# The order of the steps of attention: one turning of probabilities behind each bank of scores, third and fourth exponentials apart

## The chip, the core and the metric

One core of a Trainium2 chip. The metric is the time of one execution on the device in microseconds, median of several runs: 1551.44 us (1549.46 to 1552.54 in 3 runs). The granted TensorE clock over the span was 0.988 of full speed.

## What is computed

One inference step of a hybrid layer over 2048 prompt positions (and 128 sample positions): RMSNorm, one wide input projection, three mixers side by side (forgetting attention of 8 heads x 64, an S5 state space, memory attention of 4 heads x 64 into 256 tokens), each gated, and an output projection with a residual. The change touches only the attention of the prompt:

```
def fox_block(q, k, v, cq, ck, q_pos, k_pos):
    s = einsum('bqhd,bkhd->bhqk', q, k) * HEAD_DIM ** -0.5
    s = s + cq[..., :, None] - ck[..., None, :]          # decay of the forget gates
    p = softmax(where(k_pos[None, :] <= q_pos[:, None], s, -inf))
    return einsum('bhqk,bkhd->bqhd', p, v)
```

and the memory attention, which is the same without decay and mask. All of it is in float32 or in pairs of rounded float32 parts.

## The kernel before

`before_attention` (projections, S5, the sample positions) takes the span up to about 819 us. `attention_and_output` then runs attention to about 1348 us and the output projection to the end.

**Rounds.** A head's 16 query tiles of 128 rows are cut into 11 *rounds* (`attention_rounds`, L1859); 8 heads make 88, numbered through. In heads 0 to 6 the rounds have, in this order, query tile 12; 13; 14; 15; 8 with memory tiles 0 and 1; 9 with 2 and 3; 10 with 4 and 5; 11 with 6 and 7; 0 to 3; 4 and 5; 6 and 7. The last head (`LAST_GROUPS`) begins with the small tiles. So rounds 11 to 14 are tiles 12 to 15 of the second head, 15 to 18 its tiles 8 to 11, 19 to 21 the small ones, and 22 begins the third head. Tile t has t+1 key blocks of 128 (the mask leaves out the rest). Every round has 4 *banks* of scores, a bank being up to 4 key blocks (128x512); the blocks are then turned (transposed) in 3 or 4 *turnings* of up to 4 blocks. Rounds are paired into groups (the small ones are three), 5 per head and 40 in all, and each group's products with the values are made at once.

**Steps.** I write S(n,i) for the scores of bank i of round n, E(n,i) for its exponentials, T(n,i) for a turning, V for a group's products with the values, B for the turning back of a group's output.

- S(n,i), TensorE: L2202 and L2205, for the diagonal block L2204; for memory L2208 and L2209. It writes one of 5 banks of PSUM (`RING`), so it waits for E of five banks before: S(n,1) waits for E(n-1,0), S(n,2) for E(n-1,1), S(n,3) for E(n-1,2), S(n+1,0) for E(n-1,3). VectorE reduces each bank to its maximum (L2367) and, when a tile's banks are through, makes the negated maximum (L2371; L2360 and L2363 where one bank is all). So where a tile fills all four banks (rounds 11 to 14, and 22 on), E(n,0) cannot begin before the maximum of S(n,3); in rounds 15 to 18 it follows the third bank.
- E(n,i), ScalarE: L2291, with a row sum that is read out by a second instruction.
- T(n,i), TensorE: L2219, four transposes into one of 2 banks (`TURNS`), so it waits until the turning two before it is copied out. The copies alternate through the whole stage: even ones on ScalarE (L2301), odd ones on VectorE (L2380); rounds 19 and 20 have 3 turnings, so in round 20 the two engines change parts. So T(n-1,0) waits for ScalarE's copy of T(n-2,2), T(n-2,3) for VectorE's of T(n-2,1).
- V (L2235) on TensorE, its copy (L2307) on ScalarE, B (L2242) on TensorE, the division by the sums (L2390, L2393, L2402) on VectorE.

**The order.** `attention_order` (L1875) writes one list of steps. Each engine walks that list and takes its own part of each step, in order, with semaphore waits in front: an instruction that waits holds everything behind it on its engine. A step of scores is TensorE's matmuls and VectorE's maximum; a turning is TensorE's transposes and the copy on ScalarE or VectorE. Per iteration n the list before is

```
S(n,0) E(n-1,2) E(n-1,3) T(n-2,2) T(n-2,3) [B] [V] S(n,1) S(n,2) T(n-1,0) S(n,3) T(n-1,1) E(n,0) E(n,1)
```

V comes in the iteration three after its group's last round, B in the one after that. In the last head ScalarE also rounds the output weights, one piece ahead of T(n-1,0) and one behind E(n,1). Behind attention come the output projection's steps (`mix`, `mixed`, `product`, `y`), which the change does not touch. DMAs are issued by SyncE alone, and none is in this list; they wait for semaphores of attention's progress.

Of the kernel before, what the change touches and what calls it, by code (L numbers as in the profile page):

```python
# [1874 lines left out]
def attention_order(rounds):  # L1875


    last = {n: r.group for n, r in enumerate(rounds) if n + 1 == len(rounds) or rounds[n + 1].group != r.group}
    order = []

    def some(what, n, at):
        if 0 <= n < len(rounds):
            have = len(rounds[n].turns if what == "turn" else rounds[n].banks)
            order.extend((what, n, i) for i in at if i < have)

    first = next(n for n, r in enumerate(rounds) if r.head == FOX_HEADS - 1)
    for n in range(len(rounds) + 4):
        some("scores", n, (0,))
        some("exp", n - 1, (2, 3))
        some("turn", n - 2, (2, 3))  # L1890
        if n - 4 in last:
            order.append(("back", last[n - 4]))
        if n - 3 in last:
            order.append(("values", last[n - 3]))
        if first < n <= first + KC:
            order.append(("w_split", n - first - 1, 0))
        some("scores", n, (1, 2))
        some("turn", n - 1, (0,))
        some("scores", n, (3,))
        some("turn", n - 1, (1,))  # L1900
        some("exp", n, (0, 1))
        if first < n <= first + KC:
            order.append(("w_split", n - first - 1, 1))


        if n == len(rounds) + 1:
            order.append(("mix", 0))
            order.append(("mixed", 0))
        if n == len(rounds) + 2:
            order.append(("product", 0, 0))  # L1910
            order.append(("mix", 1))
    order += [("mixed", 1), ("product", 0, 1), ("y", 0, 0), ("y", 0, 1)]
    for o in range(1, TILES):
        order.append(("product", o, 0))
        if o + 1 < TILES:
            order += [("mix", o + 1), ("mixed", o + 1)]
        order += [("product", o, 1), ("y", o, 0), ("y", o, 1)]
    return order


def attention_and_output(nc, K, D, w_out):
# [9 lines left out]
    LANE = HD + 2  # L1931
    rounds, groups = attention_rounds()
    order = attention_order(rounds)
    SLOTS = max(sum(len(r.blocks) for r in g) for g in groups)
    bank0, turn0 = ([sum(len(x(r)) for r in rounds[:n]) for n in range(len(rounds) + 1)]
# [586 lines left out]
```

## Time and profile before

| | |
|---|---|
| median of 3 runs | 1551.44 us |
| profiled execution | 1551.53 us, of it span 1549.8 us |
| TensorE busy in the span | 1453.9 us, 94% |
| VectorE busy | 863.9 us, 56% |
| ScalarE busy | 712.5 us, 46% |

Times in rows are microseconds from the start of the span. A row of the timeline is a run of like instructions on one engine: start, time until the last one ends, engine, line, operation, the tiles written and read, shape, count, and in brackets how long the engine stood idle before it and whose result ended the idle time. A matmul's end is modelled, and matmuls overlap: four transposes take 0.60 us from the first start to the last end, but the next matmul starts 0.35 us after the first. So waits between TensorE's steps are best read from start to start.

### The profile page before, as it was taken

Reading aid. Unit: us, or ns where it says so; the run is one execution under the profiler, and the core shown is the slowest. Engines: PE = TensorE matmul, PEld = TensorE weight load, DVE = VectorE, ACT = ScalarE, POOL = GpSimd, SP = SyncE. Lnnn points to the kernel's source line nnn. Section 1 sums busy time; section 2 is a strip of 40 time slices with the busy share of each in tenths; the row PEclk is TensorE's granted clock in tenths of the full one; section 3 lists DMA queues with packets and bytes.
Section 4 is the critical chain, followed back from the end, with each engine's and each line's share of the span. In section 5 each row is a group of like instructions: output and inputs, shape, how many; then the busy total and the mean of one; then the engine's idle time right before and its main releaser. Section 6 shows DMA issues by size and latency. Waiting matters only on the chain. (4 is left out here: it accounts for less than half of the span.)

```text
span 1549.8 us, 28675 instructions
## 1 busy us (share of the span) xinstructions
PE 1453.9 (94%) x10318; PEld 1196.5 (77%) x10318; DVE 863.9 (56%) x1873; ACT 712.5 (46%) x1726; POOL 215.4 (14%) x294
## 2 busy tenths in 40 slices
PE   7999997999989989999997999999999999899998
PEld 7998766778767767777776777877778787788887
DVE  3689754772557776663325666666666665422221
ACT  5666422432524543453325665666666667500100
POOL 1110442100133332220001000000000003221110
PEclk9999998999999999999998999999999999999999
DMA  7785799695398596779868545062451602155543
GB/s 223 237 268 202 253 251 238 204 310 171 96 251 270 184 264 218 258 247 329 271 202 190 158 87 124 22 144 53 92 117 29 144 2 63 56 177 174 183 153 105
DMA packets 207676, 271.86 MB, mean 175 GB/s; under 512 B 73456, under 2 KB 147600, under 8 KB 203920
## 3 DMA queue, kind: packets, MB, share of 16 engines
q1 hardware_dynamic: 206496, 270.02, 59.7%
q8 instruction: 84, 1.38, 0.4%
q14 instruction: 56, 0.46, 0.1%
q10 hardware_dynamic: 1040, 0.00, 0.0%
HBM read 184.83 MB, written 83.90 MB: 173 GB/s over the span
## 5 line engine op out<-in xcount | busy, mean ns | idle before, releaser
L910 PE MATMUL in_g<-in_wh,in_xh 128*128 128x512 f32 (+2 forms) x904 | 333.8, 382 | 16.3 <-DVE in_wl L1478 5.8
L910 PE MATMUL in_g<-in_wl,in_xh 128*128 128x512 f32 (+2 forms) x904 | 323.3, 371 | 0.0
L2367 DVE TENSOR_REDUCE attn_tops<-attn_s 128x1 f32<-128x512 f32 (+3 forms) x288 | 171.5, 618 | 142.5 <-PE attn_s L2205 141.4
L2291 ACT ACTIVATE attn_probs<-attn_s,attn_negmax 128x512 f32<-128x512 f32 (+3 forms) x384 | 224.3, 601 | 30.9 <-DVE attn_negmax L2371 30.9
L910 PE MATMUL in_g<-in_wh,in_xl 128*128 128x512 f32 (+2 forms) x904 | 236.3, 380 | 1.4 <-DVE in_xl L1502 1.3
L2219 PE MATMUL attn_t<-all_ident,attn_probs 128*128 128x128 f32 x1216 | 192.9, 278 | 36.0 <-ACT attn_probs_turned L2301 21.9
L910 PEld LDWEIGHTS in_g<-in_wh,in_xh 128*128 128x128 f32 x904 | 166.5, 190 | 53.9 <-issue 21.1
L2219 PEld LDWEIGHTS attn_t<-all_ident,attn_probs 128*128 128x128 f32 x1216 | 144.5, 142 | 79.3 <-issue 31.2
L910 PEld LDWEIGHTS in_g<-in_wl,in_xh 128*128 128x128 f32 x904 | 166.7, 190 | 28.3
L910 PEld LDWEIGHTS in_g<-in_wh,in_xl 128*128 128x128 f32 x904 | 159.1, 190 | 34.9 <-issue 5.2
L2301 ACT ACTIVATE attn_probs_turned<-attn_t 128x512 f32<-128x512 f32 x168 | 99.9, 594 | 83.4 <-PE attn_t L2219 83.4
L2235 PE MATMUL attn_pv<-attn_probs_turned,attn_v 128*64 128x128 f32 x2176 | 134.6, 275 | 0.9 <-DVE attn_out L2402 0.7
L2235 PEld LDWEIGHTS attn_pv<-attn_probs_turned,attn_v 128*64 128x64 f32 x2176 | 125.1, 137 | 7.1 <-issue 5.6
L1196 ACT ACTIVATE in_xh<-in_xu 128x512 fp32r<-128x512 f32 x174 | 99.6, 622 | 43.3 <-DMA in_xu<-scratch_xt 38.0
L2380 DVE COPY attn_probs_turned<-attn_t 128x512 f32<-128x512 f32 (+3 forms) x168 | 100.5, 598 | 14.4 <-PE attn_t L2219 12.7
L2268 PE MATMUL attn_s<-wout_lo,attn_qa 128*128 128x512 f32 x272 | 106.0, 390 | 0.0
L2327 ACT ACTIVATE attn_qa<-attn_s 128x512 fp32r<-128x512 f32 (+1 forms) x34 | 14.8, 488 | 162.3 <-PE attn_s L2254 162.3
L1780 POOL TENSOR_TENSOR in_hv<-in_hs,all_neghalf 128x8 f32<-128x8 f32 (+1 forms) x53 | 85.9, 1620 | 4.4
L1502 DVE TENSOR_TENSOR in_xl<-in_xu,in_xh 128x512 fp32r<-128x512 f32 x106 | 68.6, 688 | 25.7 <-ACT in_xh L1196 25.5
L2291 ACT ACTIVATION_READ_ACCUMULATOR attn_probs<-attn_s,attn_negmax 128x1 f32 x384 | 80.1, 209 | 0.0
L1778 POOL TENSOR_SCALAR in_hs<-in_hs 128x8 f32<-128x8 f32 (+1 forms) x53 | 22.2, 419 | 407.7 <-DVE in_hs L1529 407.7
L2202 PE MATMUL attn_s<-all_ka,all_qa 128*128 128x512 f32 (+3 forms) x160 | 70.9, 443 | 7.6 <-PEq L72 6.4
(288 smaller groups left out, 2337.7 us busy)
## 6 DMA issues: line engine op xcount, KB each, us to landing
in_xu<-scratch_xt SPq DMA_DIRECT2D x87, 512.0 KB, 4.8
in_xl<-scratch_xt SPq DMA_DIRECT2D x34, 512.0 KB, 4.6
in_raw<-in_w_in SPq DMA_DIRECT2D x40, 256.0 KB, 5.5
scratch_xt<-in_xu SPq DMA_DIRECT2D x19, 512.0 KB, 5.3
scratch_xt<-in_xl SPq DMA_DIRECT2D x17, 512.0 KB, 6.2
scratch_k<-in_x_turned SPq DMA_DIRECT2D x17, 512.0 KB, 6.0
scratch_q<-in_x_turned SPq DMA_DIRECT2D x17, 512.0 KB, 5.3
in_x_turned<-in_x_prompt SPq DMA_DIRECT2D x16, 512.0 KB, 4.9
```

Of the source, the lines that this page charges most:

```text
L910: last = X.matmul(g_ps[b][:, 0:m], x, ws[:, c, w0:w0 + m], start=(c == 0 and h == 0 and ws is wh), stop=(c == KC - 1 and h == 1))
L1196: F(xh[:, item_visit[j] % 2, 4 * h:4 * h + 4, :], xu[:, j % 2, 4 * h:4 * h + 4, :], ACT.Copy)\
L1502: V.tensor_tensor(xl[:, v % 3, 4 * h:4 * h + 4, :], xu[:, j % 2, 4 * h:4 * h + 4, :], fl(xh[:, v % 2, 4 * h:4 * h + 4, :]), ALU.subtract). ...
L1780: G.tensor_tensor(hv[:, 0:m], hs[:, 0:m], K.neghalf[:, 0:m], ALU.pow).then_inc(s_hchain, 1)
L2202: X.matmul(bank[:, at:at + n, :], qa[h][:, q], ka[h][:, keys], start=True, stop=False)
L2219: last = X.transpose(t_ps[q % TURNS][:, j, :], probs[:, s % 2, i, at, :], K.ident[:, :])
L2235: last = X.matmul(v_ps[lane * HD:(lane + 1) * HD, j, :], vals[:, k, :], pt[:, s % 2, slots[lane, k], :], start=k == 0, stop=(lane, k + 1) ...
L2268: last = X.matmul(y_ps[h], ms[:, o % 2, c, :], ws, start=(c == 0 and k == 0), stop=(c == KC - 1 and k == 2))
L2291: last = F(probs[:, s % 2, i, at:at + n, :], s_ps[g % RING][:, at:at + n, :], ACT.Exp, bias=negmax[:, s % 2, top:top + 1], accum_out=total)
L2301: F(pt[:, r.group % 2, at:at + n, :], t_ps[q % TURNS][:, 0:n, :], ACT.Copy).then_inc(s_read_a, 1)
L2367: V.tensor_reduce(tops[:, s % 2, i:i + 1], bank[:, 0:n, :].rearrange("p n k -> p (n k)"), AX.X, ALU.max).then_inc(s_top, 1)
L2380: V.tensor_copy(pt[:, r.group % 2, at:at + n, :], t_ps[q % TURNS][:, 0:n, :]).then_inc(s_read_v, 1)
```

## The change

```diff
@@ def attention_order(rounds):
     for n in range(len(rounds) + 4):
         some("scores", n, (0,))
-        some("exp", n - 1, (2, 3))
-        some("turn", n - 2, (2, 3))
+        some("exp", n - 1, (2,))
+        some("turn", n - 2, (2,))
+        some("scores", n, (1,))
+        some("exp", n - 1, (3,))
+        some("turn", n - 2, (3,))
         if n - 4 in last:
             order.append(("back", last[n - 4]))
         if n - 3 in last:
             order.append(("values", last[n - 3]))
         if first < n <= first + KC:
             order.append(("w_split", n - first - 1, 0))
-        some("scores", n, (1, 2))
+        some("scores", n, (2,))
         some("turn", n - 1, (0,))
         some("scores", n, (3,))
         some("turn", n - 1, (1,))
```

The list of an iteration becomes

```
S(n,0) E(n-1,2) T(n-2,2) S(n,1) E(n-1,3) T(n-2,3) [B] [V] S(n,2) T(n-1,0) S(n,3) T(n-1,1) E(n,0) E(n,1)
```

On TensorE S(n,1) moves ahead of T(n-2,3), B and V. On ScalarE the copy of T(n-2,2) moves ahead of E(n-1,3). On VectorE the maximum of S(n,1) moves ahead of the copy of T(n-2,3) and of B's division. No instruction is added or taken away, and no wait's condition changes.

## Rows read from the trace of the kernel before

**Rows 1.** The page: busy time by engine; TensorE in 40 slices; its group of turnings

```profile
PE 1453.9 (94%) x10318; PEld 1196.5 (77%) x10318; DVE 863.9 (56%) x1873; ACT 712.5 (46%) x1726; POOL 215.4 (14%) x294
...
PE   7999997999989989999997999999999999899998
...
L2219 PE MATMUL attn_t<-all_ident,attn_probs 128*128 128x128 f32 x1216 | 192.9, 278 | 36.0 <-ACT attn_probs_turned L2301 21.9
```

**Rows 2.** Stretches: length; busy (count) of PE, PEld, DVE, ACT, POOL; clock; DMA

```profile
840.00:1340.00 500.00, 463.78 (x4479) 390.08 (x4476) 316.97 (x718) 328.49 (x956) 20.84 (x10) 1.00 0.39 88
905.00:970.00 65.00, 60.34 (x583) 50.68 (x584) 41.54 (x95) 41.87 (x124) 0.00 (x0) 1.00 0.41 88
```

**Rows 3.** TensorE's waits, 840 to 1340 us: us in total, times, longest

```profile
PE attn_t L2219 <- ACT attn_probs_turned L2301: 20.3, 30, 1.7
PE attn_t L2219 <- DVE attn_probs_turned L2380: 9.4, 27, 0.8
PE attn_s L2202 <- ACT attn_probs L2291: 1.7, 7, 0.3
```

**Rows 4.** Timeline, end of iteration 14 and iteration 15, up to V

```profile
902.03 0.47 PE L2202 MATMUL attn_s<-attn_ka,attn_qa 128*128 128x512 f32 x1
...
902.71 0.60 PE L2219 MATMUL attn_t<-all_ident,attn_probs 128*128 128x128 f32 x4
...
902.90 0.69 DVE L2367 TENSOR_REDUCE attn_tops<-attn_s 128x1 f32<-128x512 f32 x1 [0.75 <-PE attn_s L2205]
...
903.06 0.48 PE L2202 MATMUL attn_s<-attn_ka,attn_qa 128*128 128x512 f32 x1
...
903.61 0.60 PE L2219 MATMUL attn_t<-all_ident,attn_probs 128*128 128x128 f32 x4
...
903.82 0.69 ACT L2291 ACTIVATE attn_probs<-attn_s,attn_negmax 128x512 f32<-128x512 f32 x1 [0.92 <-DVE attn_negmax L2371]
...
904.41 0.19 ACT L2291 ACTIVATION_READ_ACCUMULATOR attn_probs<-attn_s,attn_negmax 128x1 f32 x1
...
904.55 0.52 PE L2219 MATMUL attn_t<-all_ident,attn_probs 128*128 128x128 f32 x3 [0.33 <-DVE attn_probs_turned L2380]
...
905.00 3.28 PE L2235 MATMUL attn_pv<-attn_probs_turned,attn_v 128*64 128x128 f32 x54
```

**Rows 5.** Timeline, iterations 16 and 17, up to V

```profile
910.18 0.68 ACT L2291 ACTIVATE attn_probs<-attn_s,attn_negmax 128x512 f32<-128x512 f32 x1
...
910.88 1.36 PE L2219 MATMUL attn_t<-all_ident,attn_probs 128*128 128x128 f32 x8
...
911.85 0.49 ACT L2291 ACTIVATE attn_probs<-attn_s,attn_negmax 128x256 f32<-128x256 f32 x1
...
912.28 0.69 DVE L2380 COPY attn_probs_turned<-attn_t 128x512 f32<-128x512 f32 x1 [0.21 <-PE attn_t L2219]
...
912.66 0.28 PE L2202 MATMUL attn_s<-attn_ka,attn_qa 128*128 128x256 f32 x1
...
912.75 0.62 ACT L2301 ACTIVATE attn_probs_turned<-attn_t 128x512 f32<-128x512 f32 x1
...
913.52 0.63 PE L2219 MATMUL attn_t<-all_ident,attn_probs 128*128 128x128 f32 x4 [0.34 <-ACT attn_probs_turned L2301]
...
914.72 0.69 ACT L2291 ACTIVATE attn_probs<-attn_s,attn_negmax 128x512 f32<-128x512 f32 x1
...
916.34 3.71 PE L2235 MATMUL attn_pv<-attn_probs_turned,attn_v 128*64 128x128 f32 x62
```

**Rows 6.** Timeline of TensorE, two further waits of this head

```profile
925.70 0.63 PE L2219 MATMUL attn_t<-all_ident,attn_probs 128*128 128x128 f32 x4 [0.53 <-ACT attn_probs_turned L2301]
...
946.88 0.51 PE L2202 MATMUL attn_s<-all_ka,all_qa 128*128 128x512 f32 x1 [0.23 <-ACT attn_probs L2291]
```

**Rows 7.** TensorE's longest wait of the stage, on the timeline

```profile
1294.02 0.98 PE L2219 MATMUL attn_t<-all_ident,attn_probs 128*128 128x128 f32 x4 [1.73 <-ACT attn_probs_turned L2301]
```

**Rows 8.** The stretch behind that wait, columns as in rows 2

```profile
1294.00:1297.40 3.40, 3.38 (x15) 3.10 (x16) 1.34 (x2) 2.76 (x8) 0.56 (x1) 0.52 0.20 80
```

## The prediction

> **What bounds the kernel now.** The page comes first: TensorE is busy 94% of the span, VectorE 56%, ScalarE 46% [rows 1]. Attention's steady part, 840 to 1340 us, is 463.8 of 500 us busy on TensorE at full clock, against 317 and 328 us on the other two [rows 2]. So TensorE is the bound, and what an order of steps can win is the time in which it stands. The table of waits says what it stands for: 20.3 us in 30 waits of a turning for ScalarE's copy, 9.4 us in 27 for VectorE's copy, and only 1.7 us of scores waiting for exponentials [rows 3]. A matmul's modelled end hides part of every wait: the turning of 913.52 is listed with 0.34 us idle, yet the scores before it begin at 912.66 and fill 0.28 us, so it is 0.58 us late [rows 5]. Four turnings take 0.60 us [rows 4] and one lasts 0.28 [rows 1], so they follow each other at (0.60 - 0.28) / 3 = 0.11 us; the eight at 910.88 should take 7 x 0.11 + 0.28 = 1.05 us and take 1.36, so a wait of 0.3 us hides there with no bracket at all [rows 5]. One head period, 905 to 970, holds by such starts about 7.5 us of standing, though its busy sum leaves only 4.7 us [rows 2]. That 7.5 us is an estimate from reading every step's start once round the head.
>
> The Trainium skill, Perfetto Trace Analysis, section Identifying the Most-Contended Engine, warns that matmul occupancy is no good measure of what TensorE has left. The trace agrees: 7.5 against 4.7 us in this head. By the busy sum alone all eight heads would have 37 us to give, by the starts 60 us; neither is my sum, which comes from the walk below.
>
> **The change part by part.** Every instruction stays; three moves are made, and none is a DMA's. SyncE's queue and POOL's are not in the list and are not passed; their waits fall earlier with attention's progress.
>
> *Move 1, ScalarE's copy of T(n-2,2) ahead of E(n-1,3).* In iteration 16, E(15,3) starts at 911.85 (two exponentials of 256) and the copy of T(14,2) only at 912.75; it ends at 913.37 and T(15,0) starts 0.15 us later [rows 5]. Moved, the copy starts at 911.87 and ends at 912.48, so T(15,0) may start at 912.63, 0.9 us earlier. With one bank of 512 in E(n-1,3), the move is worth one exponential, 0.69 us [rows 4]. E(15,3) ends where the copy ended before; its takers, S(17,0) and T(15,3), come three steps later on TensorE, so nothing waits. ScalarE is now held by the copy if the turning is late, but T(14,2) is done about 0.4 us before the copy is due, and in none of the walks below is it late.
>
> *Move 2, S(n,1) ahead of T(n-2,3).* This gives VectorE time to copy T(n-2,1), which is the 0.3 us in the row of eight and the 0.33 us of 904.55 [rows 4, 5]. But S(n,1) needs the bank that E(n-1,0) reads. Before, T(n-2,3), B and V stood between, and V alone is 3.2 us (54 products, 3.28 us to the last one's end [rows 4]). Now only S(n,0) and T(n-2,2) do. Where a tile fills four banks the chain is: S(14,3) at 902.03, its maximum from 902.90, E(14,0) 903.82 to 904.60 [rows 4]. TensorE would be ready for S(15,1) at 903.61 + 0.38 = 903.99 and gets its bank at 904.65: a new wait of 0.66 us, in place of the old one, which ended at 904.55.
>
> *Move 3, on VectorE,* the maximum of S(n,1) goes ahead of the copy of T(n-2,3) and the division behind B. The work is the same, begun earlier; S(n,2)'s maximum now follows the division, which I put at 1.1 us for a group of eight tiles (an estimate: one pass over 128x512, 0.69 us as the maximum of 902.90 [rows 4], and two short ones ahead), and E(n,0) follows that.
>
> *The walk, V to V.* V is long enough for ScalarE and VectorE to empty their queues, so each stretch between two V can be walked alone, and the results added. I take the rows' times, put the steps in the new order, and let each start at the latest of: the step before it on its engine (a bank of 512 scores 0.55 us, from 903.06 to 903.61; four turnings 0.35, from 902.71 to 903.06, to 0.38 before scores, 4 x 0.11 before turnings [rows 4]), the copy's end + 0.15 [rows 5], the exponential's end + 0.05 (my estimate for a wait that the rows barely show).
>
> Stretch of iterations 16 and 17 [rows 5]. T(14,2) at 910.88. S(16,1) could start at 911.26; E(15,0), from 910.18, ends with its read-out 0.78 us later (as 903.82 to 904.60 [rows 4]), at 910.96, so it does. T(14,3) 911.81, B, S(16,2) 912.30, T(15,0) 912.63 rather than 913.52. VectorE: the maximum of S(16,1) begins 0.77 us after its start (0.87 from 902.03 to 902.90 less the 0.10 of the diagonal block [rows 4]), at 912.03, then copy, division and maximum of S(16,2) follow without a gap, the same work that before began at 912.28; so E(16,0) starts at 914.5 rather than 914.72 and ends at 915.28. TensorE: S(16,3) 913.0, T(15,1) 913.57, S(17,0) 913.93, T(15,2) 914.48; ready at 914.86, S(17,1) waits until 915.33. T(15,3) 915.88, V 916.12 rather than 916.34. S(17,1) is already done, which took 0.57 us behind V before. Gain 0.22 + 0.57 = 0.8 us. So 0.9 us are freed at T(15,0) and 0.3 at T(14,3), and 0.47 us are lost again at S(17,1).
>
> Stretch of iterations 14 and 15. S(14,3), at 902.03 in rows 4, comes 0.55 us earlier, but VectorE, with a division of 1.1 us between, makes E(14,0) only 0.3 us earlier, 903.5 to 904.3. S(15,1) 904.33, T(13,3) 904.88, V 905.33, its successor S(15,2) at 905.33 + 3.2 = 908.53, where before it stood at 905.00 + 3.2 + 0.57 = 908.77: gain 0.25 us. Each head has one such stretch.
>
> The other three, walked alike: iterations 18 and 19, where T(17,0) waits for ScalarE at 925.70 [rows 6], gain 1.1; 20 and 21, 0.45; 22 to 24, about -0.1. In the last, B and V stood before S(22,1), which still started only when E(21,0) was done (946.88 [rows 6]); now B's 0.33 us comes behind that wait instead of within it, and the later waits win 0.27 us back.
>
> Sum per head 0.8 + 0.25 + 1.1 + 0.45 - 0.1 = 2.5 us. Of the 7.5 us of standing, 5 stay, 4.3 of it in front of S(·,1). Eight heads: 20 us; I take 2.45, the unrounded sum, so 19.6 us. The last head has other neighbours but the same round shapes. Behind attention TensorE is busy 8 to 9 tenths of every slice with the output projection [rows 1], and its loads wait for attention's own semaphores, so the gain passes through.
>
> Against the profiled execution, 1551.5 us (0.1 above the median of 1551.44), this is 1531.9. I forecast **1532 us**.
>
> Bounds. Above: if all listed waits went, 31.4 us [rows 3], and the half clock of 1294 to 1297.4 too. There TensorE stood 1.73 us for ScalarE's copy behind two exponentials of 256 and ran 3.4 us at 0.52 of its clock [rows 7, 8]; the copy now comes 0.9 us earlier. That is worth at most half of 3.4, 1.7 us. I do not count it, and do not expect the whole of the waits; low end 1524. Below: the rivals.
>
> **Rivals.**
>
> *A, the forecast:* 1532 us, chance 0.60.
>
> *B, the wait only changes its place.* The bank of E(n-1,0) sets the pace everywhere as it does in iteration 15, and the earlier copy merely lets TensorE reach S(n,1) sooner. For it: E(14,0) already waits 0.92 us on its maximum [rows 4]. Against: in iterations 16 to 21 E(n,0) hangs on the third bank and on ScalarE's queue, which move 1 shortens. Then each V stretch wins what 14 and 15 win or less, 0.15: 40 stretches, 6 us: 1545.5. Chance 0.22.
>
> *C, slower: S(n,1) in front of V starves TensorE.* V used to cover the chain S(n-1,3), maximum, E(n-1,0). Now five times per head TensorE must sit it out before V may begin, and VectorE's division makes the chain longer in the iterations with B. My walk has 4.3 us of such waits per head, 0.39 per iteration. From 6.75 us per head, 0.61 per iteration, the change loses. The 0.66 us of iteration 15 lies on that side, and so does any VectorE that comes 0.3 us later than walked. At 0.67 us per iteration in all 88: 88 x 0.06 = 5 us slower, 1556.5. Chance 0.10.
>
> *D, the clock.* A long stand cost half clock once, at 1294 [rows 7, 8]; the other 29 of that kind, 0.64 us each in the mean, did not: (20.3 - 1.7) / 29 [rows 3]. If the new waits before S(n,1), up to 1 us in iteration 26, set it off, each costs up to 1.7 us. The Trainium skill, TensorE: Matmul & The Clock Gate, section A second HAM failure mode, describes just this, short idle gaps between groups that cycle PSUM banks; here the clock held at 1.00 through 500 us with 57 listed waits on turnings [rows 2, 3]. Six such falls: 10 us given back, 1542; twelve would eat the gain. Chance 0.08.
>
> That the change does not do what it says (the copy held by a late T(n-2,2)) would be B's time.
>
> **How the numbers follow.** About 0.2%, 3.1 us, is what a measurement of this kernel can tell from no change. Faster by more: all of A, most of B (0.19 of 0.22), most of D (0.06): 0.85. The same: 0.05. Slower: 0.10, C. The range runs from 1524 to 1547: it takes in B and most of D, and leaves out C and a gain of over 27 us.
>
> **What would show it.** T waiting for ScalarE's copy falls from 20.3 us to under 6; T waiting for VectorE's from 9.4 to under 3; S waiting for exponentials rises from 1.7 to 15 to 30 us. Attention, 529 us before (819 to 1348), would take about 509, and no other stretch changes its length. The prediction is wrong in its step if S's waits exceed 40 us, or if the clock falls below 1.00 in new places.

## The result and the profile after

The changed kernel takes 1533.69 us (median; 1531.68 to 1535.54, 4 runs) against 1551.45 for the kernel before (4 runs): ratio 0.9884, 95% interval 0.9864 to 0.9904, 17.8 us faster. On another chip, in a later comparison, it was 1531.18 against 1548.48: 0.9887 (0.987 to 0.9903). The forecast was 1532 us, with a range of 1524 to 1547.

The page of the changed kernel first: busy time by engine, TensorE in 40 slices, and the group of turnings, which answer to rows 1.

```profile
PE 1452.1 (95%) x10318; PEld 1199.1 (78%) x10318; DVE 860.7 (56%) x1873; ACT 714.0 (47%) x1726; POOL 216.8 (14%) x294
...
PE   7999997999998989999997999999999999999998
...
L2223 PE MATMUL attn_t<-all_ident,attn_probs 128*128 128x128 f32 x1216 | 190.7, 275 | 5.8 <-ACT attn_probs_turned L2305 4.3
```

No engine has fewer instructions; the turnings' listed idle time fell from 36.0 us [rows 1] to 5.8. (The lines of `kernel.py` stand 4 lower after the change: L2206 and L2209 are scores, L2223 turnings, L2239 V.) TensorE's waits in 840 to 1340 us, as in rows 3:

```profile
PE attn_s L2206 <- ACT attn_probs L2295: 17.0, 39, 0.8
PE attn_t L2223 <- ACT attn_probs_turned L2305: 3.8, 9, 0.7
PE attn_t L2223 <- DVE attn_probs_turned L2384: 0.9, 1, 0.9
```

Both waits on copies are nearly gone, 29.7 us to 4.7, and 17.0 us of scores waiting for exponentials stand in their place, in 39 waits where there were 7 [rows 3]. The granted clock was 1.00 throughout, with 475.7 of 500 us busy on TensorE where there were 463.8 [rows 2]:

```profile
840.00:1340.00 500.00, 475.67 (x4608) 403.92 (x4608) 320.14 (x734) 334.95 (x969) 22.83 (x12) 1.00 0.40 91
```

The timeline of the changed kernel shows where the new waits stand, here in iterations 14 and 15, which answer to rows 4:

```profile
900.33 0.15 DVE L2394 TENSOR_REDUCE attn_den<-attn_dens 128x4 f32<-128x8 f32 x1
...
900.75 0.69 DVE L2406 TENSOR_TENSOR attn_out<-attn_pv,attn_rden 128x512 f32<-128x512 f32 x1
...
900.92 0.47 PE L2206 MATMUL attn_s<-attn_ka,attn_qa 128*128 128x512 f32 x1
...
901.36 1.28 DVE L2371 TENSOR_REDUCE attn_tops<-attn_s 128x1 f32<-128x512 f32 x2
...
902.67 0.16 DVE L2375 TENSOR_REDUCE attn_negmax<-attn_tops 128x1 f32<-128x4 f32 x1
...
902.87 0.69 ACT L2295 ACTIVATE attn_probs<-attn_s,attn_negmax 128x512 f32<-128x512 f32 x1 [1.06 <-DVE attn_negmax L2375]
...
903.70 0.50 PE L2206 MATMUL attn_s<-attn_ka,attn_qa 128*128 128x512 f32 x1 [0.60 <-ACT attn_probs L2295]
...
904.69 0.55 PE L2239 MATMUL attn_pv<-attn_probs_turned,attn_v 128*64 128x128 f32 x6
```

S(14,3) starts at 900.92 and its maximum could be taken 0.87 us later, at 901.79, as before [rows 4]. VectorE, held by the division (900.33 to 901.44) and then by the maximum of S(14,2), comes to it at about 901.96. E(14,0) follows at 902.87, and S(15,1) at 903.70, after 0.60 us of listed idle time, before V may begin. This profile's attention began 1.8 us later (S(0,0) at 820.65 us instead of 818.85), in work that the change does not touch. One stretch of that work, 3.4 us from 224.66, ran at half clock (0.50), which it did not in the profile before; why is open.

### The profile page after: what moved, and what is told of

It is laid out like the page before. It is cut to its first block and busy times, and to the rows that moved or that the text cites. A ratio compares the mean times of both kernels' runs of the same rounds, so it can differ in the third digit from the quotient of the medians.

```text
span 1533.7 us, 28675 instructions
## 1 busy us (share of the span) xinstructions
PE 1452.1 (95%) x10318; PEld 1199.1 (78%) x10318; DVE 860.7 (56%) x1873; ACT 714.0 (47%) x1726; POOL 216.8 (14%) x294
## 5 line engine op out<-in xcount | busy, mean ns | idle before, releaser
L2295 ACT ACTIVATE attn_probs<-attn_s,attn_negmax 128x512 f32<-128x512 f32 (+3 forms) x384 | 227.7, 605 | 38.5 <-DVE attn_negmax L2375 38.3
L2223 PE MATMUL attn_t<-all_ident,attn_probs 128*128 128x128 f32 x1216 | 190.7, 275 | 5.8 <-ACT attn_probs_turned L2305 4.3
L2223 PEld LDWEIGHTS attn_t<-all_ident,attn_probs 128*128 128x128 f32 x1216 | 147.3, 141 | 40.2 <-issue 9.2
L2239 PE MATMUL attn_pv<-attn_probs_turned,attn_v 128*64 128x128 f32 x2176 | 134.6, 275 | 0.8 <-DVE attn_out L2406 0.7
L2239 PEld LDWEIGHTS attn_pv<-attn_probs_turned,attn_v 128*64 128x64 f32 x2176 | 125.0, 137 | 8.7 <-issue 8.7
L2206 PE MATMUL attn_s<-all_ka,all_qa 128*128 128x512 f32 (+3 forms) x160 | 74.3, 464 | 16.0 <-ACT attn_probs L2295 9.2
L2206 PE MATMUL attn_s<-attn_ka,attn_qa 128*128 128x512 f32 (+3 forms) x160 | 72.6, 454 | 9.5 <-ACT attn_probs L2295 8.7
```

The lines of the kernel that those rows point to most:

```text
L2206: X.matmul(bank[:, at:at + n, :], qa[h][:, q], ka[h][:, keys], start=True, stop=False)
L2223: last = X.transpose(t_ps[q % TURNS][:, j, :], probs[:, s % 2, i, at, :], K.ident[:, :])
L2239: last = X.matmul(v_ps[lane * HD:(lane + 1) * HD, j, :], vals[:, k, :], pt[:, s % 2, slots[lane, k], :], start=k == 0, stop=(lane, k + 1) ...
L2295: last = F(probs[:, s % 2, i, at:at + n, :], s_ps[g % RING][:, at:at + n, :], ACT.Exp, bias=negmax[:, s % 2, top:top + 1], accum_out=total)
```

## The experiments

TensorE's own stretches tell more than the totals. The table gives, for each kernel, the distance in us from the start of S(n,2) of an iteration with a V to that of the next one, in the second to the sixth head, where it repeats to about 0.1 us (but for one stretch of d and one of f in the fifth head, which are left out here and told at the end); "one head" is their sum, the median and the ratio are of all comparable runs. The experiments ran on three chips, where the kernel before took 1550.07 (a to d), 1551.56 (e, f, g) and 1548.48 us (h, i), so the ratios, each to the kernel before on the same chip, compare better than the medians. Stretches are named by their iterations in the second head. For instance in the changed kernel S(15,2) and S(17,2) start at

```profile
907.89 0.33 PE L2206 MATMUL attn_s<-attn_ka,attn_qa 128*128 128x128 f32 x1
...
918.90 0.45 PE L2206 MATMUL attn_s<-attn_ka,attn_qa 128*128 128x384 f32 x1
```

and 918.90 - 907.89 = 11.01.

| kernel | 14-15 | 16-17 | 18-19 | 20-21 | 22-24 | one head | median | ratio to before (95%) |
|---|---|---|---|---|---|---|---|---|
| before | 12.81 | 11.77 | 11.86 | 11.00 | 17.42 | 64.86 | 1551.45 | 1 |
| the change | 12.59 | 11.01 | 10.96 | 10.81 | 17.55 | 62.92 | 1533.69 | 0.9884 (0.9864 to 0.9904) |
| a, copy only | 12.25 | 11.72 | 11.38 | 11.00 | 17.1 | 63.45 | 1540.24 | 0.9926 (0.991 to 0.9942) |
| b, scores only | 13.00 | 11.46 | 11.50 | 10.83 | 17.9 | 64.7 | 1545.78 | 0.9979 (0.9969 to 0.9989) |
| c, change, B late | 12.44 | 10.75 | 10.74 | 11.18 | 16.67 | 61.78 | 1525.25 | 0.9846 (0.9833 to 0.9859) |
| d, scores behind V | 12.42 | 11.42 | 11.31 | 10.70 | 17.38 | 63.23 | 1537.22 | 0.9917 (0.9906 to 0.9929) |
| e, before, B late | 13.40 | 12.13 | 12.01 | 11.98 | 16.85 | 66.37 | 1561.72 | 1.0075 (1.0063 to 1.0088) |
| f, mix | 12.83 | 10.64 | 10.73 | 10.80 | 16.55 | 61.55 | 1526.61 | 0.985 (0.9836 to 0.9864) |
| h, mix again | 12.41 | 10.64 | 10.74 | 10.78 | 16.55 | 61.1 | 1521.69 | 0.9826 (0.9811 to 0.9841) |

**a: ScalarE's copy alone.** Against the changed kernel:

```diff
         some("turn", n - 2, (2,))
-        some("scores", n, (1,))
         some("exp", n - 1, (3,))
...
-        some("scores", n, (2,))
+        some("scores", n, (1, 2))
```

> The changed kernel with S(n,1) back behind V: only ScalarE's copy of T(n-2,2) stays ahead of E(n-1,3). My theory (the waits are chained through VectorE, so the copy pays only where VectorE itself stood): walked alone per head, stretch 14-15 gains 0.7 us, 16-17 nothing (VectorE works without a gap from 912.28 to 915.96 in the kernel before, so T(15,3) and V stay where they were), 18-19 0.4, 20-21 nothing, 22-24 0.5; 1.6 us per head, about 13 us in all, 1538.5 us. T's waits for ScalarE's copy under 5 us, T's waits for VectorE's copy still about 9 us. Rival 'the copy is the whole change': as fast as the changed kernel, 1533 to 1534. Rival 'each move is worth its listed wait': 20 us, 1531.

1540.24 us, 9.8 below before on that chip (1550.07). The rival that the copy is the whole change (1533 to 1534) is out. The head gains 1.4 us where 1.6 was expected: 0.56, 0.05, 0.48, 0 and 0.3. T's waits went over to VectorE's copy; the third row is T(15,3):

```profile
PE attn_t L2222 <- DVE attn_probs_turned L2383: 15.9, 36, 0.8
PE attn_t L2222 <- ACT attn_probs_turned L2304: 7.0, 17, 0.8
...
919.00 0.30 PE L2222 MATMUL attn_t<-all_ident,attn_probs 128*128 128x128 f32 x1 [0.57 <-DVE attn_probs_turned L2383]
```

In 16-17 the copy of T(14,2) starts 0.9 us earlier behind S(15,2) than before. T(15,0) comes only 0.5 us earlier (4.25 us behind S(15,2), before 4.74), because it then waits for nothing but its place behind S(16,2). Nearly all of that is spent again at T(15,3). The wait on ScalarE came out a little above the 5 us expected, the one on VectorE well above 9, which is the chain through VectorE shown more plainly than I had asked.

**b: the scores alone.** Against the changed kernel:

```diff
-        some("exp", n - 1, (2,))
+        some("exp", n - 1, (2, 3))
         some("turn", n - 2, (2,))
         some("scores", n, (1,))
-        some("exp", n - 1, (3,))
         some("turn", n - 2, (3,))
```

> The changed kernel with E(n-1,2) and E(n-1,3) together again ahead of T(n-2,2): only S(n,1) ahead of T(n-2,3), B and V stays. My theory: T's wait for ScalarE's copy stays at about 20 us, the wait for VectorE's copy goes, S(n,1) waits for E(n-1,0). Walked per head: 14-15 loses 0.1, 16-17 gains 0.4, 18-19 0.6, 20-21 0.2, 22-24 loses 0.4: 0.7 us per head, 5 to 6 us in all, 1546. Rival C of the prediction (S(n,1) in front of V starves TensorE and only the copy pays): slower than before, 1552 to 1557. Rival 'each move is worth its listed wait': 9 us, 1542.

1545.78 us, 4.3 below before: close to the walk, and neither rival. By head it is only 0.2 us instead of 0.7, with the signs as walked (-0.2, 0.3, 0.4, 0.2, -0.5). The attention stage of its trace is 2.1 us shorter than before, so half of the 4.3 us was not found in the trace.

Alone the two moves give 1.4 and 0.2 us per head, together 1.94. The difference comes from 16-17, where they give 0.05 and 0.31 alone and 0.76 together; in 14-15 they give 0.15 less together than alone. The traces show why in 16-17: kernel a still waits at T(15,3) for VectorE's copy (0.57 us, above), kernel b at T(15,0) for ScalarE's,

```profile
912.28 0.63 PE L2222 MATMUL attn_t<-all_ident,attn_probs 128*128 128x128 f32 x4 [0.65 <-ACT attn_probs_turned L2304]
```

and the changed kernel has neither wait there.

**d: S(n,1) behind V.** Against the changed kernel, in iterations with a V only:

```diff
-        some("scores", n, (1,))
+        if n - 3 not in last:
+            some("scores", n, (1,))
...
             order.append(("values", last[n - 3]))
+        if n - 3 in last:
+            some("scores", n, (1,))
```

> The changed kernel, but in the iterations that have a V, S(n,1) goes behind V again (as in the kernel before); in the others it stays ahead of T(n-2,3). Tells whether the wait of S(n,1) in front of V costs or only stands in another's place. My theory: per head iteration 15 gains 0.1, 17 loses 0.25, 19 loses 0.45, 21 nothing, 24 gains 0.1; 0.5 us per head, 4 us slower than the changed kernel, about 1538. Rival C (V is needed as a cover for the chain to E(n-1,0)): faster than the changed kernel by 5 us or more.

1537.22 us, 3.5 slower than the change by the medians, 5 by the ratios to the kernel before (0.9917 against 0.9884 and 0.9887). Rival C is out: over a head, the wait of S(n,1) in front of V costs less than what stood there. Where the round before V is a large or a small one (14-15, 20-21, 22-24) S(n,1) is 0.1 to 0.2 us better behind V; where that round has memory tiles, 0.4 worse. The signs are as walked (20-21 was walked as nothing), the sum is 0.3 us per head instead of 0.5.

**c: B late.** Against the changed kernel:

```diff
-        if n - 4 in last:
-            order.append(("back", last[n - 4]))
...
         some("turn", n - 1, (1,))
+        if n - 4 in last:
+            order.append(("back", last[n - 4]))
         some("exp", n, (0, 1))
```

> The changed kernel with B (turning back of the output, and VectorE's division behind it) moved from ahead of V to behind T(n-1,1), so the division no longer stands between the maxima of S(n,1) and S(n,2). My theory says that in the changed kernel E(n,0) hangs on VectorE in the iterations with B, and S(n+1,1) on E(n,0). Walked: stretch 14-15 gains 0.3 us, 16-17 0.4, 18-19 0.4, 20-21 0.1, 22-24 0.5, so at most 1.7 us per head; since V may then wait for the division I expect two thirds of it, 9 us below the changed kernel, about 1525. S waiting for exponentials falls well under 17 us. Rival 'ScalarE's queue, not VectorE, sets E(n,0)': within 2 us of the changed kernel. Rival 'V waits for the division instead': slower than the changed kernel, V's waits for attn_out over 5 us.

1525.25 us. Taken by the ratios, 0.9846 against 0.9884 and 0.9887, that is 6 us below the change, not 9; the heads gain 1.14 us each, as two thirds of 1.7, but the last one loses 0.6. The waits of scores for exponentials fall to 7.1:

```profile
PE attn_t L2223 <- ACT attn_probs_turned L2305: 7.9, 17, 0.8
PE attn_s L2206 <- ACT attn_probs L2295: 7.1, 17, 0.8
PE attn_pv L2239 <- DVE attn_out L2406: 3.7, 8, 0.7
```

So VectorE, held by the division, does set E(n,0) in the changed kernel. In 20-21 the late division costs more than it gives (11.18 against 10.81): there V now waits 0.43 us in each head. The third row holds six of these waits and two of the last head.

**e: B late in the kernel before.**

```diff
         some("exp", n - 1, (2, 3))
         some("turn", n - 2, (2, 3))
-        if n - 4 in last:
-            order.append(("back", last[n - 4]))
...
         some("turn", n - 1, (1,))
+        if n - 4 in last:
+            order.append(("back", last[n - 4]))
```

> The kernel before with B and VectorE's division moved behind T(n-1,1), and nothing of the change. It tells whether the division was a limit by itself or only becomes one once the copy is early. My theory: in the kernel before E(n,0) hangs on ScalarE's copy of T(n-1,0), which hangs on T(n-1,0)'s own wait, in most iterations with B, so VectorE's earlier work finds little: stretch 16-17 gains 0.3 us by T(15,3), 22-24 0.3, the rest nothing, 3 to 5 us in all, 1546. Rival 'the division is the limit by itself': as much as it gave the changed kernel, 8 to 9 us, 1541.

1561.72, 10.2 slower: both expectations were wrong. The stretch of iterations 14 and 15 in this kernel shows what I had left out:

```profile
902.33 0.48 PE L2202 MATMUL attn_s<-attn_ka,attn_qa 128*128 128x512 f32 x1
...
902.88 1.02 PE L2219 MATMUL attn_t<-all_ident,attn_probs 128*128 128x128 f32 x7
904.42 0.84 PE L2235 MATMUL attn_pv<-attn_probs_turned,attn_v 128*64 128x128 f32 x11 [0.52 <-DVE attn_out L2402]
```

V overwrites the bank that the division reads. With B late, only S(15,0) and two turnings stand between, and V waits, 12.4 us in 22 waits over the stage:

```profile
PE attn_t L2219 <- ACT attn_probs_turned L2301: 22.3, 29, 1.6
PE attn_pv L2235 <- DVE attn_out L2402: 12.4, 22, 0.9
```

In c, S(n,1) stands there too and covers the division, in all stretches of a head but one. The same edit is worth 6 us on one order and costs 10 on the other.

**f and h: the mix.** Each stretch gets the order that had been best for it; h has this, with `early` as in its second form:

```diff
+        early = n < len(rounds) and rounds[n].tiles[0].t == 4                  # f
+        early = (n - 2 in last and n < len(rounds)
+                 and all(x.kind == "fox" for x in rounds[n].tiles))            # h
+        behind = (n - 3 in last and n - 1 < len(rounds)
+                  and all(x.kind == "fox" for x in rounds[n - 1].tiles))
         some("scores", n, (0,))
         some("exp", n - 1, (2,))
         some("turn", n - 2, (2,))
-        some("scores", n, (1,))
+        if not behind:
+            some("scores", n, (1,))
         some("exp", n - 1, (3,))
         some("turn", n - 2, (3,))
-        if n - 4 in last:
+        if early and n - 4 in last:
             order.append(("back", last[n - 4]))
         if n - 3 in last:
             order.append(("values", last[n - 3]))
+        if behind:
+            some("scores", n, (1,))
...
         some("turn", n - 1, (1,))
+        if not early and n - 4 in last:
+            order.append(("back", last[n - 4]))
```

> The changed kernel with, stretch by stretch, the order that was best in the four runs: B late except in the iteration of tiles 4 and 5, where V waited for the division; S(n,1) behind V again where a V follows a round without memory tiles. If the stretches between two V are independent, as my walk assumes, each takes its best measured length or less: 12.25, 10.75, 10.74, 10.70 and 16.6 us, 61.0 us per head against 61.8 of B late and 62.9 of the change: 6 us below B late, about 1519. Rival 'the stretches are coupled': no better than B late, 1525.

1526.61 us, ratio 0.985 where c has 0.9846: no better than B late, as the rival said. But four of the five stretches came out within 0.1 us of the list; the loss is in 14-15, which took 12.83. With S(15,1) behind V nothing covered the late division, as in e:

```profile
900.48 0.77 PE L2246 MATMUL attn_pv<-attn_probs_turned,attn_v 128*64 128x128 f32 x10 [0.51 <-DVE attn_out L2413]
```

> The mix with one thing mended: B stays early wherever the next iteration begins with a V behind a round without memory tiles (iterations 14 and 20), since in the mix V waited 0.7 us for VectorE's division there. So stretch 14-15 has exactly the order of the run with the copy alone, 12.25 us, where the mix took about 12.8; the others stay at 10.64, 10.73, 10.8 and 16.6. Theory: the stretches add once B and V's wait are counted to the right one: 61.0 us per head, 6 us under B late, about 1519 to 1520. Rival 'the stretches are coupled': 1524 to 1526 as the mix and B late.

1521.69 us, 9.5 below the change on the same chip (1531.18) and 26.8 below before: the fastest kernel of this study. It is 2 us above the forecast of 1519 to 1520, and the rival that the stretches are coupled (1524 to 1526) is out. 14-15 took 12.41, not the 12.25 of a, though its steps are a's; iteration 13 in front of it is not. The stretches are nearly independent, not wholly.

> The changed kernel as it is, on the same chip as the mix, for a direct comparison: 1533 to 1534, and its seven heads take 438.6 us in the trace as in its first profile.

1531.18 us, two or three below the forecast, as was the kernel before on that chip; the seven heads took 439.2 us instead of 438.6, and the second to sixth repeat the table's 62.9.

**g: one swap.** In the kernel before, one iteration of 92:

```diff
+        if n == 81:
+            some("exp", n - 1, (2,))
+            some("turn", n - 2, (2,))
+            some("exp", n - 1, (3,))
+            some("turn", n - 2, (3,))
+        else:
...
```

> The kernel before with ScalarE's copy of T(79,2) ahead of E(80,3) in iteration 81 alone; this is the iteration whose wait of 1.7 us was followed by 3.4 us at half clock. If the wait is what set it off, the stretch at half clock is gone from attention, and the distance from S(81,2) to S(82,2), 11.4 us before, is 9.1 to 9.3: 0.8 us of the wait and 1.5 of the clock. Rival 'the clock falls there whatever the order': 10.6. In the total 2 us, 1548, at the edge of what can be measured.

TensorE in that iteration, the swapped kernel:

```profile
1291.01 0.29 PE L2208 MATMUL attn_s<-attn_ka,attn_qa 128*128 128x256 f32 x1
...
1292.35 0.63 PE L2225 MATMUL attn_t<-all_ident,attn_probs 128*128 128x128 f32 x4 [0.82 <-ACT attn_probs_turned L2307]
...
1300.26 0.34 PE L2208 MATMUL attn_s<-attn_ka,attn_qa 128*128 128x384 f32 x1
```

The wait is 0.82 instead of 1.73 us [rows 7], the four transposes behind it take 0.63 instead of 0.98, and there is no half clock there nor anywhere else in attention behind its first 11 us. From S(81,2) to S(82,2) it is 1300.26 - 1291.01 = 9.25 us; in the kernel before these steps are

```profile
1291.77 0.28 PE L2202 MATMUL attn_s<-attn_ka,attn_qa 128*128 128x256 f32 x1
...
1303.19 0.33 PE L2202 MATMUL attn_s<-attn_ka,attn_qa 128*128 128x384 f32 x1
```

and 1303.19 - 1291.77 = 11.42. Of these 2.2 us, 0.9 is the shorter wait (the turning starts 2.25 us behind S(81,2) before and 1.34 here), and 1.3 is left for the clock. In the total 1548.99 against 1551.56, ratio 0.999 (0.998 to 1.0), is at the edge of what can be measured; the 2.2 us are read from the traces.

Kernel b, which leaves that copy late, has the wait and the half clock (0.50 of full speed) at the same step:

```profile
1291.20:1294.60 3.40, 3.39 (x14) 3.16 (x15) 1.25 (x2) 2.65 (x7) 0.55 (x1) 0.50 0.50 161
1291.21 1.09 PE L2222 MATMUL attn_t<-all_ident,attn_probs 128*128 128x128 f32 x4 [1.59 <-ACT attn_probs_turned L2304]
```

So has e, which leaves it late too: it waits 1.61 us at this step, and the granted clock is 0.50 for 3.4 us from 1303.12.

```profile
1302.38 0.63 PE L2219 MATMUL attn_t<-all_ident,attn_probs 128*128 128x128 f32 x4 [1.61 <-ACT attn_probs_turned L2301]
```

None of the kernels with the early copy has it there.

## Why the prediction was right

**The bound.** Right: TensorE stands for copies, and the listed idle time understates it. By starts, the attention stage went from 525.5 us (S(0,0) to the last V) to 507.6.

**Move 1.** Right as a mechanism, a little too large. In the walk T(15,0) came 0.9 us earlier. Measured from S(15,2), it came 0.7 us earlier in the changed kernel (4.03 us behind, before 4.74) and 0.5 in a, where VectorE's copy takes it back in 16-17. What it is worth alone, 1.4 us per head, is three quarters of the change.

**Move 2.** Right. The wait for E(n-1,0) takes the place of the wait for VectorE's copy; in 14-15 V began at 904.69 with S(15,1) already done. The waits of S for exponentials were forecast at 15 to 30 us and are 17.0; those on copies under 6 and 3 and are 3.8 and 0.9.

**Move 3.** Right as a mechanism: c shows that the division in front of S(n,2)'s maximum holds up E(n,0). Its price, some 6 us, was in the walk, but I had not asked what moving it would give.

**The walk.** Forecast and measured gain per stretch: 0.25 and 0.22; 0.8 and 0.76; 1.1 and 0.90; 0.45 and 0.19; -0.1 and -0.13. Together 2.45 and 1.94 us. The term that was mis-sized is 20 and 21, less than half of what I took. Its steps, all with short banks and diagonal blocks, follow each other a little more slowly in the trace than walked: from S(19,2) to S(21,2) 10.82 us, where I had 10.55. Most of the rest is in 18 and 19, 0.20 us, whose cause was not looked for.

**The sum.** Seven heads gave 14.4 us (453.05 to 438.64 from S(2,2) to S(79,2)), not 17.2. The last head gave 3.65 us (from S(79,2) to the last V, 60.93 to 57.28), not 2.45, because the half clock at 1294, which I named and did not count, went away: 2.3 us from S(81,2) to S(82,2), of which g gives 0.9 to the wait and 1.3 to the clock. So two errors partly cancelled, one of -2.8 us and one of +1.2, and in that a total that is 2 us off was lucky.

**The rivals.** B would have given 6 us: out. C is out by the result, and d shows why. D did not come: with waits of up to 0.8 us listed before S(n,1), attention of the changed kernel has no half clock behind its first 11.6 us, which stood at half clock before too (11.1 us). A fall would have cost 1.3 us by g, not the 1.7 that D allowed. The Trainium skill, TensorE: Matmul & The Clock Gate, section A second HAM failure mode: psum-queue depth-cycling, tells of a kernel whose short idle gaps between groups that cycle PSUM banks made the clock go up and down. Here they did not: 39 listed waits of 17.0 us in all left it at 1.00 from 840 to 1340 us. Whether longer ones in such number would is not shown.

## What to carry to other kernels

Where several engines walk one list in order, move one step and then ask which engine's own queue sets the next release: here ScalarE's copy moved 0.9 us (a, 16-17) and the gain was decided by what VectorE had in front of a maximum. Stretches between two long steps that drain the other queues can be walked alone from the rows, and added. But an edit's worth belongs to the order around it: B late gave 6 us on one order and cost 10 on the other, since one step of scores more or less covered it.

## What the runs showed of the hardware

**The clock.** TensorE stood for 1.73 us [rows 7], for 1.59 us (b) and for 1.61 us (e) in full-speed work and then ran 3.4 us at half clock, which began at the end of the stand, in e 0.7 us behind it. In d it stood 1.89 us for nothing that the profile shows, at 1084.75, with the same sequel, and that one stretch took 15.57 us where its fellows took 12.4:

```profile
1084.90:1088.30 3.40, 3.40 (x14) 2.83 (x14) 1.41 (x3) 1.47 (x4) 0.00 (x0) 0.51 1.04 215
1084.75 0.98 PE L2226 MATMUL attn_t<-all_ident,attn_probs 128*128 128x128 f32 x4 [1.89 <-issue]
```

Waits of 0.82 (g), 1.07 (e, T(13,0) at 900.48) and 1.30 us (e, at 1330.12) had no such sequel. At the step where d stood, in the same head, f stood too, for less and without the sequel; its stretch took 13.83 us instead of 12.83:

```profile
1077.38 0.66 PE L2230 MATMUL attn_t<-all_ident,attn_probs 128*128 128x128 f32 x4 [0.77 <-issue]
```

Neither stand was repeated on purpose, and their cause stays open.

**The part in front.** Before a run's total is compared to 0.1%, its first 819 us must be looked at: attention began between 815.4 and 823.8 us in the profiles of these kernels, in work that is the same in all of them.
